# Transposing the normalized activations by DMA instead of TensorE in a hybrid attention and Fourier block

## The chip, the cores and the metric

The kernel runs as one program on all 8 cores of one Trainium2 chip. The time of a run is the device time of the slowest core, in microseconds (us). The cores do not talk to each other: core c computes sequence c of the first batch, and a quarter (2048 tokens) of one of the two longer sequences of the second.

## The reference, cut to what matters

```python
def _mixer_layer(x, ln_w, w_in, q_norm, k_norm, w_f, b_f, w_out):
    h = _rmsnorm(x, ln_w)                              # (B, S, 1024)
    proj = jnp.einsum("bsd,de->bse", h, w_in)          # 1024 -> 2304
    q, k, v, g_a, u_f, g_f = jnp.split(proj, SPLITS, axis=-1)   # 512 128 128 512 512 512
    q = _apply_rope(_rmsnorm(q.reshape(B, S, 8, 64), q_norm), cos, sin)
    k = _apply_rope(_rmsnorm(k.reshape(B, S, 2, 64), k_norm), cos, sin)
    y_attn = _block_attention(q, k, v) * jax.nn.silu(g_a)       # full softmax over S
    y_four = _fourier_mix(u_f, w_f, b_f) * jax.nn.silu(g_f)     # real(fft2), then 128x128 per group
    y = jnp.concatenate([y_attn, y_four], axis=-1)
    return x + jnp.einsum("bse,ed->bsd", y, w_out)
# y_prompt = rmsnorm(_mixer_layer(x_prompt (8, 4096, 1024))), y_sample the same of (2, 8192, 1024)
```

## The kernel before, in words

Each core does two jobs one after the other: job s (S = 8192, its own 2048 query tokens) and job p (S = 4096, all tokens its own). A job has three stages with a barrier between them.

**Pass 1** (L615 to L655) goes over all S tokens in tiles of 128 (64 tiles in job s, 32 in job p), in pairs. Per tile: SP loads 512 KB of x (L623) into one of three buffers xt; ScalarE squares and sums it (L478) and makes the reciprocal root in two tiny steps (L482, L483); VectorE scales it to bf16, hb (L626). The projection needs the model dimension on the partitions, so TensorE transposes hb in eight 128x128 blocks through the identity matrix into a PSUM bank (L631), and VectorE copies the bank to hT (L633). Then eight steps, each a 256-column matmul for K and V (L637) and a 512-column one for the Fourier input U (L640). ScalarE takes U and V out of PSUM (L642, L643). Per pair of tiles the K part goes through `normrope`: square on ScalarE (L498), sum on VectorE (L499), two tiny ScalarE steps (L501, L502), two VectorE products (L503, L506), six GpSimd steps (L517 to L522). TensorE transposes the result, kb (L652, two blocks), and VectorE copies it to kT (L654). GpSimd loads the rotary table of a pair (L618).

**Fourier** (L662 to L716) works from U in SBUF. The change does not touch it.

**Attention** first loads and converts w_out and w_in, then works in chunks of 512 queries (4 in job s, 8 in job p). `part_a` of a chunk normalizes four tiles of x (L797, L480 to L483, L800), transposes them (L809) and copies them (L811) into the four quarters of hTc, of which there is one; projects Q (L814), normalizes and rotates it and transposes it (L825, L829); then makes the gates (L839, exponentials and the reciprocal L847). Job s takes its tiles singly, job p in pairs. `part_b` is the attention itself: per key tile two score matmuls (L864, L866), one exponential of 1024 columns (L872), two value matmuls (L878, L880), and at the end of each of four head pairs a normalization on VectorE and GpSimd (L884 to L892). `part_c` is the output projection (L920), the residual, the last norm and the store (L929). part_a of the next chunk and part_c of the last run as a background stream beside part_b.

**The order of the work** is written by a planner, `Prog.schedule`. The operations of a stage are entered with the buffers that they read and write; each engine's queue is then laid out by a list schedule with fixed charges: it takes the operation that can start first, among equals the one of lower due time, then the one entered first. The emitted queues are run in that order, each engine waiting on semaphores where needed; nothing is reordered on the chip. DMAs are charged on one serial resource for all queues:

```python
if sid == 1 and e == "pe":
    rdy += BG_SLACK                      # 2.0: background TensorE work is planned 2 us late
...
if o.dma:
    xs = max(stt, dma_free)
    dma_free = xs + o.nbytes / 150000.0
    o.t1 = dma_free + 2.0
    free[o.eng] = stt + o.c
```

The charges of compute are n/2400 + 0.03 us on TensorE, (n + 335)/1200 on ScalarE, (n + 150)/960 on VectorE and 0.003 n + 0.15 on GpSimd, with 0.15 us for a hop between engines. A buffer is a whole: a write to any quarter of hTc waits for every read of hTc entered before it. A DMA of a queue also waits for the eighth DMA before it on that queue.

Of the kernel before, what the change touches and what calls it, by code (L numbers as in the profile page):

```python
# [8 lines left out]
BF16 = mybir.dt.bfloat16  # L9
# [5 lines left out]
D = 1024  # L15
# [341 lines left out]
def build(stop=None):  # L357
# [64 lines left out]
    def bank(i, n=1):  # L422
        return psum[:, 512 * i:512 * (i + n)]
# [121 lines left out]
    def run_job(job):  # L545
# [36 lines left out]
        w1 = AF_.get((8, 768), BF16)  # L582
        NXT = 3
        xt = [AF_.get((1024,), F32) for _ in range(NXT)]
        hb = [AF_.get((1024,), BF16) for _ in range(2)]
        hT = [AF_.get((8, 128), BF16) for _ in range(2)]
        junk = AF_.get((1024,), BF16)
        st_s = [AF_.get((4,), F32) for _ in range(2)]
        rt = [AF_.get((2, 64), F32) for _ in range(2)]
# [10 lines left out]
        B_w1, B_U = Buf(), Buf()  # L600
        B_xg = [Buf(), Buf()]
        B_xt = [Buf() for _ in range(NXT)]
        B_hb, B_hT, B_st, B_rt, B_kb = ([Buf(), Buf()] for _ in range(5))
        B_junk = Buf()
        B_p12 = [Buf() for _ in range(NS1)]
        B_stage = [Buf() for _ in range(NSTG)]
# [8 lines left out]
        for jp in range(J // 2):  # L615
            bkv = 2 + (jp % 2)
            rts = jp % 2
            P.op("pool", lambda e, jp=jp, rts=rts: e.dma_start(out=rt[rts], in_=rk[nm][2 * jp:2 * jp + 2].rearrange("t p c -> p t c")),  # L618
                 writes=[B_rt[rts]], dma=True, nbytes=65536)
            for tl in range(2):  # L620
                j = 2 * jp + tl
                xs_, hs = j % NXT, j % 2
                P.op("sp", lambda e, j=j, xs_=xs_: e.dma_start(out=xt[xs_], in_=x_str[j]), writes=[B_xt[xs_]], dma=True, nbytes=524288)  # L623
                ss, lnv, rstd = st_s[hs][:, 0:1], st_s[hs][:, 1:2], st_s[hs][:, 2:3]
                rms_rstd(xt[xs_], B_xt[xs_], junk, B_junk, ss, lnv, rstd, B_st[hs], D)
                P.op("dve", lambda e, xs_=xs_, hs=hs, rstd=rstd: e.tensor_scalar(hb[hs], xt[xs_], rstd, None, ALU.mult),  # L626
                     reads=[B_xt[xs_], B_st[hs]], writes=[B_hb[hs]], n=600)
                bt = j % 2
                psT = bank(bt).bitcast(BF16)
                for kc in range(8):  # L630
                    P.op("pe", lambda e, kc=kc, hs=hs, psT=psT: e.transpose(psT[:, kc * 128:(kc + 1) * 128], hb[hs][:, kc * 128:(kc + 1) * 128], ident),  # L631
                         reads=[B_hb[hs], B_ident], writes=[PB[bt]], n=128)
                P.op("dve", lambda e, hs=hs, psT=psT: e.tensor_copy(hT[hs].rearrange("p a b -> p (a b)"), psT),  # L633
                     reads=[PB[bt]], writes=[B_hT[hs]], n=700)
                bu = 4 + (j % 3)
                for kc in range(8):
                    P.op("pe", lambda e, kc=kc, hs=hs, tl=tl, bkv=bkv: e.matmul(bank(bkv)[:, tl * 256:(tl + 1) * 256], hT[hs][:, kc, :], w1[:, kc, 0:256],  # L637
                                                                       start=(kc == 0), stop=(kc == 7)),
                         reads=[B_hT[hs], B_w1], writes=[PB[bkv]], n=256)
                    P.op("pe", lambda e, kc=kc, hs=hs, bu=bu: e.matmul(bank(bu), hT[hs][:, kc, :], w1[:, kc, 256:768], start=(kc == 0), stop=(kc == 7)),  # L640
                         reads=[B_hT[hs], B_w1], writes=[PB[bu]], n=512)
                P.op("act", lambda e, j=j, bu=bu: e.activation(U[:, j, :], bank(bu), AF.Copy), reads=[PB[bu]], writes=[B_U], n=512)  # L642
                P.op("act", lambda e, j=j, tl=tl, bkv=bkv: e.activation(  # L643
                    vx[:, j, :].rearrange("p (a b) -> p a b", b=64)[:, 0:3:2, :],
                    bank(bkv)[:, tl * 256 + 128:(tl + 1) * 256].rearrange("p (a b) -> p a b", b=64), AF.Copy),
                    reads=[PB[bkv]], writes=[B_vx[j]], n=128)
            ksrc = bank(bkv).rearrange("p (t c) -> p t c", t=2)[:, :, 0:128]
            kslot = jp % 2
            normrope(ksrc, [PB[bkv]], 2, 2, gk, rt[rts], B_rt[rts], kb[kslot], B_kb[kslot], wkk[kslot])
            psK = bank(7).bitcast(BF16)  # L650
            for tl in range(2):
                P.op("pe", lambda e, tl=tl, kslot=kslot, psK=psK: e.transpose(psK[:, tl * 128:(tl + 1) * 128], kb[kslot][:, tl * 128:(tl + 1) * 128], ident),  # L652
                     reads=[B_kb[kslot], B_ident], writes=[PB[7]], n=128)
            P.op("dve", lambda e, jp=jp, psK=psK: e.tensor_copy(kT[:, jp * 256:(jp + 1) * 256], psK[:, 0:256]),  # L654
                 reads=[PB[7]], writes=[B_kT[2 * jp], B_kT[2 * jp + 1]], n=256)  # L655
# [125 lines left out]
        def part_a(ch):  # L781
            P.strm = 1
            cs = ch % 2
            for tp in range(4 // TP):
# [5 lines left out]
                for tl in range(TP):  # L790
                    t = tp * TP + tl
                    tg = ch * 4 + t
                    xs_, hs = cnt["x"] % 2, tg % 2
                    cnt["x"] += 1
                    sts = cnt["st"] % 4
                    cnt["st"] += 1
                    P.op("sp", lambda e, tg=tg, xs_=xs_: e.dma_start(out=xt2[xs_], in_=x_nat[tg]), writes=[B_xt2[xs_]], dma=True, nbytes=524288)  # L797
                    ss, lnv, rstd = st2[sts][:, 0:1], st2[sts][:, 1:2], st2[sts][:, 2:3]
                    rms_rstd(xt2[xs_], B_xt2[xs_], junk2, B_junk2, ss, lnv, rstd, B_st2[sts], D, sq_eng="dve")
                    P.op("dve", lambda e, xs_=xs_, hs=hs, rstd=rstd: e.tensor_scalar(hb2[hs], xt2[xs_], rstd, None, ALU.mult),  # L800
                         reads=[B_xt2[xs_], B_st2[sts]], writes=[B_hb2[hs]], n=600)
                    if TP == 1:
                        ba, bb = 6 + (t % 2), 7 - (t % 2)
                    else:
                        ba = bb = 6 + tl
                    banks.append(bb)
                    psT = bank(ba).bitcast(BF16)
                    for kc in range(8):
                        P.op("pe", lambda e, kc=kc, hs=hs, psT=psT: e.transpose(psT[:, kc * 128:(kc + 1) * 128], hb2[hs][:, kc * 128:(kc + 1) * 128], ident),  # L809
                             reads=[B_hb2[hs], B_ident], writes=[PB[ba]], n=128)  # L810
                    P.op("dve", lambda e, t=t, psT=psT: e.tensor_copy(hTc[:, :, t * 128:(t + 1) * 128], psT.rearrange("p (a b) -> p a b", a=8)),  # L811
                         reads=[PB[ba]], writes=[B_hTc], n=700)
                    for kc in range(8):
                        P.op("pe", lambda e, kc=kc, t=t, bb=bb: e.matmul(bank(bb), hTc[:, kc, t * 128:(t + 1) * 128], w2[:, kc, 0:512], start=(kc == 0), stop=(kc == 7)),  # L814
                             reads=[B_hTc, B_w2], writes=[PB[bb]], n=512)
# [208 lines left out]
```

How the kernel before makes its waits and increments, by code:

```python
                def body(eng):  # L259
                    seen = {}
                    for o in ops:
                        need = {}
                        for d in o.deps:
                            if d.dma:
                                k = ("d",) + d.dsem
                                v = d.dcnt
                                sem = dsem[d.dsem]
                            else:
                                k = ("c", d.eng)
                                v = d.cnt
                                sem = esem[d.eng]
                            if seen.get(k, 0) >= v:
                                continue
                            if k not in need or need[k][1] < v:
                                need[k] = (sem, v)
                        for k, (sem, v) in need.items():
                            eng.wait_ge(sem, v)
                            seen[k] = v
                        ins = o.fn(eng)
                        if o.dma:
                            ins.then_inc(dsem[o.dsem], 16)
                        elif o.sig:
                            ins.then_inc(esem[e], 1)
                    if e == "sp":
                        for k, sem in dsem.items():
                            if dcount[k] > 0:
                                eng.wait_ge(sem, dcount[k])
```

## Time and profile before

| | us |
|---|---|
| median of 2 runs | 3724.66 |
| the two runs | 3652.83, 3796.48 |
| the profiled execution | 3620.57 |
| its span on the slowest core (7) | 3619.0 |
| spans of the 8 cores in it | 3577.8 to 3619.0 |

| engine (core 7) | busy us | share of the span |
|---|---|---|
| TensorE | 2982.6 | 82% |
| ScalarE | 2448.5 | 68% |
| VectorE | 1856.3 | 51% |
| GpSimd | 859.3 | 24% |
| DMA | | mean 45 GB/s |

The profile is of one execution on its slowest core. A group of instructions is named by its source line. "L652 waited for L522" means that the semaphore that released L652 was raised by L522. The granted clock (PEclk) is the TensorE clock as a share of its full speed, 2.4 GHz. Matmuls are pipelined, and their starts are a better guide than their durations: a matmul's record overlaps the next one's.

### The profile page before, as it was taken

To read this page: it belongs to the slowest core of one execution; us is meant where nothing else is said; L and a number is where in the kernel's file an instruction comes from. 1 tells how busy PE (TensorE), PEld (TensorE's weight loads), DVE (VectorE), ACT (ScalarE), POOL (GpSimd) and SP (SyncE) were. 2 spreads that over 40 slices of the span, in tenths; PEclk is the share of its full clock that TensorE was granted. 3 is DMA by queue.
4 is the path that set the end of the run, shared out by engine and by line. 5 is a ranking of instruction groups with operands and counts; after the bars stand their busy time and mean duration, and the time that the engine had idled before them with its cause. 6 is when DMAs were issued, how large, how long until landed. Compare 5 with 4: busy or idle time off the path is not lost.

```text
span 3619.0 us, 51220 instructions; the slowest of 8 cores (3577.8 to 3619.0 us)
## 1 busy us (share of the span) xinstructions
PE 2982.6 (82%) x15376; PEld 1067.2 (29%) x15376; DVE 1856.3 (51%) x2072; ACT 2448.5 (68%) x3409; POOL 859.3 (24%) x1119
## 2 busy tenths in 40 slices
PE   5885651799999999999576642999999999999997
PEld 3553430222222222222143421222222222222221
DVE  3555764633235235311345435765767575757553
ACT  4661220499998998999454640778777878786875
POOL 4556772220002002000145532111111202020100
PEclk8996655899999999999798765999999999988887
DMA  5540005000010010000241023001020111101011
GB/s 153 144 138 14 1 1 156 21 2 1 24 36 14 18 41 13 18 30 1 88 138 48 1 68 99 13 7 65 4 68 30 43 41 32 59 14 59 12 47 35
DMA packets 49547, 162.86 MB, mean 45 GB/s; under 512 B 7088, under 2 KB 9168, under 8 KB 49280
## 3 DMA queue, kind: packets, MB, share of 16 engines
q1 hardware_dynamic: 41536, 138.43, 12.1%
q0 software_dynamic: 7744, 21.15, 2.0%
q8 instruction: 133, 2.18, 0.2%
q14 instruction: 134, 1.10, 0.1%
HBM read 134.39 MB, written 25.17 MB: 44 GB/s over the span
## 4 chain that ended last, share of the span: by engine, by line
PE 64%; DVE 15%; issue 7%; POOL 6%; ACT 4%; DMA 3%; DVEq 0%; POOLq 0%; ACTq 0%; SPq 0%
PE psum L864 16%; PE psum L878 16%; PE psum L880 11%; PE psum L920 5%; DVE arena L847 4%; PE psum L640 3%; PE psum L839 3%; PE psum L814 2%; PE psum L637 2%; DVE arena L676 1%; DVE arena L678 1%; POOL arena L680 1%; POOL arena L682 1%; DMA arena<-w_in 1%; ACT arena L709 1%
## 5 line engine op out<-in xcount | busy, mean ns | idle before, releaser
L872 ACT ACTIVATE arena<-psum 128x1024 bf16<-128x1024 f32 x2048 | 1959.6, 1060 | 296.0 <-PE psum L866 227.3
L878 PE MATMUL psum<-arena 128*128 128x512 bf16 x2048 | 815.6, 399 | 25.4 <-DVE arena L884 24.0
L864 PE MATMUL psum<-arena 64*128 64x512 bf16 x2048 | 794.9, 389 | 49.5 <-ACT arena L872 32.2
L866 PE MATMUL psum<-arena 64*128 64x512 bf16 x2048 | 808.3, 396 | 0.0
L880 PE MATMUL psum<-arena 128*128 128x512 bf16 x2048 | 795.1, 392 | 7.1 <-DVE arena L885 7.0
L864 PEld LDWEIGHTS psum<-arena 64*128 64x128 bf16 x2048 | 188.7, 92 | 952.5 <-issue 950.4
L889 POOL TENSOR_TENSOR arena<-arena 128x512 f32<-128x512 f32 x48 | 59.5, 1239 | 1389.5 <-DVE arena L888 1389.5
L878 PEld LDWEIGHTS psum<-arena 128*128 128x128 bf16 x2048 | 196.2, 96 | 497.1 <-issue 494.6
L847 DVE RECIPROCAL arena<-arena 128x512 f32<-128x512 f32 x96 | 321.7, 3351 | 8.4
L640 PE MATMUL psum<-arena 128*128 128x512 bf16 x768 | 255.3, 381 | 0.0
L637 PE MATMUL psum<-arena 128*128 128x256 bf16 x768 | 208.1, 274 | 54.9 <-DVE arena L633 27.0
L920 PE MATMUL psum<-arena 128*128 128x512 bf16 x768 | 224.3, 403 | 32.8 <-DVE arena L892 17.9
L482 ACT ACTIVATE arena<-arena 128x1 f32<-128x1 f32 x192 | 56.6, 299 | 264.8 <-DVE arena L481 247.4
L700 ACT ACTIVATE arena<-psum 128x256 bf16<-128x256 f32 x192 | 74.9, 390 | 231.7 <-PE psum L692 181.2
L880 PEld LDWEIGHTS psum<-arena 128*128 128x128 bf16 x2048 | 203.3, 100 | 26.4 <-issue 19.9
L839 PE MATMUL psum<-arena 128*128 128x512 bf16 x768 | 199.0, 401 | 8.5 <-DVE arena L493 4.2
L884 DVE COPY arena<-psum 128x512 f32<-128x512 f32 x48 | 32.5, 676 | 323.8 <-PE psum L878 323.8
L517 POOL TENSOR_TENSOR arena<-arena 128x128 f32<-128x128 f32 (+2 forms) x80 | 57.4, 717 | 573.3 <-DVE arena L506 573.3
L866 PEld LDWEIGHTS psum<-arena 64*128 64x128 bf16 x2048 | 189.0, 93 | 7.8 <-issue 7.2
L676 DVE TENSOR_TENSOR arena<-psum,arena 128x512 f32<-128x512 f32 x192 | 133.4, 698 | 106.6 <-PE psum L671 70.4
L671 PE MATMUL psum<-arena 128*64 128x256 bf16 (+1 forms) x1024 | 121.9, 398 | 76.8 <-DVE arena L678 71.7
L927 DVE SCALAR_TENSOR_TENSOR arena<-arena 128x1024 f32<-128x1024 f32 x48 | 61.6, 1283 | 231.1 <-ACT arena L483 230.7
(106 smaller groups left out, 3661.6 us busy)
## 6 DMA issues: line engine op xcount, KB each, us to landing
arena<-xp SPq DMA_DIRECT2D x96, 512.0 KB, 3.8
arena<-xs SPq DMA_DIRECT2D x64, 512.0 KB, 5.2
arena<-xo SPq DMA_DIRECT2D x32, 512.0 KB, 3.6
yp<-arena SPq DMA_DIRECT2D x32, 512.0 KB, 2.7
arena<-w_in POOLq DMA_DIRECT2D x40, 256.0 KB, 5.5
yo<-arena SPq DMA_DIRECT2D x16, 512.0 KB, 2.7
arena<-w_in SPq DMA_DIRECT2D x24, 256.0 KB, 4.8
arena<-w_in SPq DMA_DIRECT2D x16, 128.0 KB, 3.6
```

The costliest lines, as they stand in the source:

```text
L637: P.op("pe", lambda e, kc=kc, hs=hs, tl=tl, bkv=bkv: e.matmul(bank(bkv)[:, tl * 256:(tl + 1) * 256], hT[hs][:, kc, :], w1[:, kc, 0:256], s ...
L640: P.op("pe", lambda e, kc=kc, hs=hs, bu=bu: e.matmul(bank(bu), hT[hs][:, kc, :], w1[:, kc, 256:768], start=(kc == 0), stop=(kc == 7)), rea ...
L671: P.op("pe", lambda e, bl=bl, cl=cl, cidx=cidx, b1=b1: e.matmul(bank(b1)[cl * J:(cl + 1) * J, bl * 256:(bl + 1) * 256], U.rearrange("p j c ...
L676: P.op("dve", lambda e, s1=s1, pv=pv: e.tensor_tensor(p12[s1][:, 0, :, :], pv, t1.unsqueeze(1).to_broadcast([128, 2, 256]), ALU.mult), rea ...
L839: P.op("pe", lambda e, kc=kc, fc=fc, bg=bg: e.matmul(bank(bg), w2[:, kc, 512 + fc * 128:512 + (fc + 1) * 128], hTc[:, kc, :], start=(kc == ...
L847: P.op("dve", lambda e, es=es: e.reciprocal(eg[es], eg[es]), reads=[B_eg[es]], writes=[B_eg[es]], n=3000)
L864: P.op("pe", lambda e, kt=kt, sb=sb, hp=hp: e.matmul(bank(sb), kT[0:64, kt * 128:(kt + 1) * 128], qT[cs][0:64, hp, :], start=True, stop=True),
L866: P.op("pe", lambda e, kt=kt, sb=sb, hp=hp: e.matmul(bank(sb + 1), kT[64:128, kt * 128:(kt + 1) * 128], qT[cs][64:128, hp, :], start=True, ...
L872: P.op("act", lambda e, sb=sb, ps=ps: e.activation(pT[ps], bank(sb, 2), AF.Exp, scale=0.125), reads=[PB[sb], PB[sb + 1]], writes=[B_pT[ps] ...
L878: P.op("pe", lambda e, kt=kt, ps=ps: e.matmul(bank(4), vx[:, kt, 0:128], pT[ps][:, 0:512], start=(kt == 0), stop=(kt == NKT - 1)), reads=[ ...
L880: P.op("pe", lambda e, kt=kt, ps=ps: e.matmul(bank(5), vx[:, kt, 64:192], pT[ps][:, 512:1024], start=(kt == 0), stop=(kt == NKT - 1)), rea ...
L920: P.op("pe", lambda e, c8=c8, half=half, t=t: e.matmul(bank(6 + half), yT[cs][:, c8, t * 128:(t + 1) * 128], wo[:, c8, half * 512:(half + ...
```

## The change

In pass 1 and in part_a, the eight TensorE transposes of a tile and VectorE's copy out of PSUM are replaced by one DMA on SP's queue, SBUF to SBUF, with transposition, 256 KB. In pass 1, hb and hT get three buffers each instead of two (the small statistics buffers keep two). The K and Q transposes (L652, L825) and those of the Fourier stage stay on TensorE. The planner is told nbytes=262144 for each new DMA.

```diff
-        hb = [AF_.get((1024,), BF16) for _ in range(2)]
-        hT = [AF_.get((8, 128), BF16) for _ in range(2)]
+        NHS = 3
+        hb = [AF_.get((1024,), BF16) for _ in range(NHS)]
+        hT = [AF_.get((8, 128), BF16) for _ in range(NHS)]
...
-                bt = j % 2
-                psT = bank(bt).bitcast(BF16)
-                for kc in range(8):
-                    P.op("pe", lambda e, kc=kc, hs=hs, psT=psT: e.transpose(psT[:, kc * 128:(kc + 1) * 128], hb[hs][:, kc * 128:(kc + 1) * 128], ident),
-                         reads=[B_hb[hs], B_ident], writes=[PB[bt]], n=128)
-                P.op("dve", lambda e, hs=hs, psT=psT: e.tensor_copy(hT[hs].rearrange("p a b -> p (a b)"), psT),
-                     reads=[PB[bt]], writes=[B_hT[hs]], n=700)
+                P.op("sp", lambda e, hs=hs: e.dma_start(out=hT[hs], in_=hb[hs].rearrange("p (a b) -> p a b", a=8), transpose=True),
+                     reads=[B_hb[hs]], writes=[B_hT[hs]], dma=True, nbytes=262144)
...
-                    psT = bank(ba).bitcast(BF16)
-                    for kc in range(8):
-                        P.op("pe", lambda e, kc=kc, hs=hs, psT=psT: e.transpose(psT[:, kc * 128:(kc + 1) * 128], hb2[hs][:, kc * 128:(kc + 1) * 128], ident),
-                             reads=[B_hb2[hs], B_ident], writes=[PB[ba]], n=128)
-                    P.op("dve", lambda e, t=t, psT=psT: e.tensor_copy(hTc[:, :, t * 128:(t + 1) * 128], psT.rearrange("p (a b) -> p a b", a=8)),
-                         reads=[PB[ba]], writes=[B_hTc], n=700)
+                    P.op("sp", lambda e, hs=hs, t=t: e.dma_start(out=hTc[:, :, t * 128:(t + 1) * 128], in_=hb2[hs].rearrange("p (a b) -> p a b", a=8), transpose=True),
+                         reads=[B_hb2[hs]], writes=[B_hTc], dma=True, nbytes=262144)
```

## Rows read from the trace of the kernel before

**Rows 1.** Cores: span and mean granted clock of the slowest.
```profile
core 7: 3619.0 us, clock 0.883
```

**Rows 2.** The page's chain of work that ended last, by engine.
```profile
PE 64%; DVE 15%; issue 7%; POOL 6%; ACT 4%; DMA 3%; DVEq 0%; POOLq 0%; ACTq 0%; SPq 0%
```

**Rows 3.** Stretches: start:end length, busy of PE, PEld, DVE, ACT, POOL, PEclk, DMA, GB/s.
```profile
52.00:290.00 238.00, 197.20 (x1511) 123.23 (x1509) 124.44 (x240) 150.53 (x446) 122.26 (x210) 1.00 0.45 133
290.00:545.00 255.00, 151.36 (x1216) 94.86 (x1213) 173.52 (x264) 53.39 (x103) 184.36 (x268) 0.58 0.00 1
...
670.00:1780.00 1110.00, 1068.90 (x4840) 302.68 (x4839) 402.91 (x376) 989.82 (x1125) 99.45 (x114) 0.99 0.06 19
...
1826.00:1956.00 130.00, 101.61 (x767) 62.95 (x765) 61.81 (x121) 73.54 (x218) 61.87 (x110) 0.97 0.31 105
...
2258.00:3619.00 1361.00, 1273.63 (x5668) 377.39 (x5666) 852.33 (x730) 1040.07 (x1227) 193.49 (x160) 0.92 0.11 35
```

**Rows 4.** Timeline of pass 1, 200 to 212 us: start, length, engine, line.
```profile
200.38 0.38 ACT L498 ACTIVATE arena<-psum 128x256 f32<-128x256 f32 x1
...
201.31 0.27 PE L652 MATMUL psum<-arena 128*128 128x128 bf16 x2 [0.77 <-POOL arena L522]
...
202.40 0.30 ACT L501 ACTIVATE arena<-arena 128x4 f32<-128x4 f32 x1 [0.61 <-DVE arena L499]
...
203.17 0.42 DVE L503 TENSOR_TENSOR arena<-psum,arena 128x256 f32<-128x256 f32 x1 [0.86 <-ACT arena L502]
203.26 1.06 PE L631 MATMUL psum<-arena 128*128 128x128 bf16 x16
...
204.59 0.42 DVE L506 TENSOR_TENSOR arena<-arena 128x256 f32<-128x256 f32 x1
...
204.93 0.27 PE L637 MATMUL psum<-arena 128*128 128x256 bf16 x1 [0.61 <-DVE arena L633]
...
205.22 0.45 POOL L517 TENSOR_TENSOR arena<-arena 128x128 f32<-128x128 f32 x1 [3.32 <-DVE arena L506]
...
207.20 0.27 PE L637 MATMUL psum<-arena 128*128 128x256 bf16 x1
...
208.28 0.38 ACT L498 ACTIVATE arena<-psum 128x256 f32<-128x256 f32 x1
...
209.23 0.27 PE L652 MATMUL psum<-arena 128*128 128x128 bf16 x2 [0.78 <-POOL arena L522]
```

**Rows 5.** Groups by line: shapes and count, busy us, mean ns, idle before.
```profile
L478 ACT ACTIVATE arena<-arena 128x1024 bf16<-128x1024 f32 x96 | 101.5, 1057 | 46.1 <-DMA arena<-xp 16.0 <-issue 12.8 <-DMA arena<-xs 8.3
L626 DVE TENSOR_SCALAR arena<-arena 128x1024 bf16<-128x1024 f32 x96 | 76.3, 818 | 9.2 <-ACT arena L483 9.1
L633 DVE COPY arena<-psum 128x1024 bf16<-128x1024 bf16 x96 | 65.6, 687 | 32.5 <-PE psum L631 23.4 <-PE psum L640 8.7
L811 DVE COPY arena<-psum 128x1024 bf16<-128x1024 bf16 x48 | 32.8, 683 | 30.3 <-PE psum L809 19.2 <-PE psum L814 10.8
```

**Rows 6.** Timeline of TensorE after long idle times: pass 1's first tile, then job s's prelude.
```profile
44.66 0.37 PE L637 MATMUL psum<-arena 128*128 128x256 bf16 x1 [10.46 <-DVE arena L537]
...
45.26 0.42 PE L637 MATMUL psum<-arena 128*128 128x256 bf16 x1
...
45.90 0.42 PE L637 MATMUL psum<-arena 128*128 128x256 bf16 x1
...
47.65 0.27 PE L637 MATMUL psum<-arena 128*128 128x256 bf16 x1
...
637.60 3.57 PE L814 MATMUL psum<-arena 128*128 128x512 bf16 x8 [0.68 <-DVE arena L829]
...
654.02 3.57 PE L814 MATMUL psum<-arena 128*128 128x512 bf16 x8 [0.68 <-DVE arena L829]
```

**Rows 7.** DMA: a queue (packets, MB, share of 16 engines), and issues (KB, us to landing).
```profile
q1 hardware_dynamic: 41536, 138.43, 12.1%
...
arena<-xs SPq DMA_DIRECT2D x64, 512.0 KB, 5.2
...
arena<-rq_s POOLq DMA_DIRECT2D x16, 32.0 KB, 2.0
```

More of the change, by code:

```diff
@@ L602, in run_job @@
         B_xt = [Buf() for _ in range(NXT)]
-        B_hb, B_hT, B_st, B_rt, B_kb = ([Buf(), Buf()] for _ in range(5))
+        B_st, B_rt, B_kb = ([Buf(), Buf()] for _ in range(3))
+        B_hb, B_hT = ([Buf() for _ in range(NHS)] for _ in range(2))
         B_junk = Buf()
@@ L621, in run_job @@
                 j = 2 * jp + tl
-                xs_, hs = j % NXT, j % 2
+                xs_, hs = j % NXT, j % NHS
                 P.op("sp", lambda e, j=j, xs_=xs_: e.dma_start(out=xt[xs_], in_=x_str[j]), writes=[B_xt[xs_]], dma=True, nbytes=524288)
-                ss, lnv, rstd = st_s[hs][:, 0:1], st_s[hs][:, 1:2], st_s[hs][:, 2:3]
-                rms_rstd(xt[xs_], B_xt[xs_], junk, B_junk, ss, lnv, rstd, B_st[hs], D)
+                sj = j % 2
+                ss, lnv, rstd = st_s[sj][:, 0:1], st_s[sj][:, 1:2], st_s[sj][:, 2:3]
+                rms_rstd(xt[xs_], B_xt[xs_], junk, B_junk, ss, lnv, rstd, B_st[sj], D)
                 P.op("dve", lambda e, xs_=xs_, hs=hs, rstd=rstd: e.tensor_scalar(hb[hs], xt[xs_], rstd, None, ALU.mult),
-                     reads=[B_xt[xs_], B_st[hs]], writes=[B_hb[hs]], n=600)
-                bt = j % 2
-                psT = bank(bt).bitcast(BF16)
-                for kc in range(8):
-                    P.op("pe", lambda e, kc=kc, hs=hs, psT=psT: e.transpose(psT[:, kc * 128:(kc + 1) * 128], hb[hs][:, kc * 128:(kc + 1) * 128], ident),
-                         reads=[B_hb[hs], B_ident], writes=[PB[bt]], n=128)
-                P.op("dve", lambda e, hs=hs, psT=psT: e.tensor_copy(hT[hs].rearrange("p a b -> p (a b)"), psT),
-                     reads=[PB[bt]], writes=[B_hT[hs]], n=700)
+                     reads=[B_xt[xs_], B_st[sj]], writes=[B_hb[hs]], n=600)
+                P.op("sp", lambda e, hs=hs: e.dma_start(out=hT[hs], in_=hb[hs].rearrange("p (a b) -> p a b", a=8), transpose=True),
+                     reads=[B_hb[hs]], writes=[B_hT[hs]], dma=True, nbytes=262144)
                 bu = 4 + (j % 3)
```

## The prediction, made before the changed kernel had been run

> **What bounds the kernel now.** I read the cores first: core 7 is the slowest, and all views are of it [rows 1]. Then the chain that ended last: two thirds of it is TensorE, a seventh VectorE, almost nothing transfers [rows 2]. An average over a program with six stages says little, so I cut the span by stage [rows 3]. The change touches two kinds of stage. Pass 1 (52 to 290 us for the first job, 1826 to 1956 for the second) has TensorE busy 83% and 78%, the others at most two thirds, DMA a third to under a half. Attention (670 to 1780, 2258 to 3619) has TensorE at 96% and 94% with ScalarE at 89% and 76% close behind.
>
> Then the timeline of pass 1, for one period [rows 4]. A pair of tiles takes 7.90 us (L498 at 200.38 and at 208.28), 3.95 per tile. Eight steps of L637 and L640 come every 0.324 us (204.93 to 207.20 is seven of them), 2.6 us a tile; the eight transposes of a tile are 0.53 (sixteen in 1.06). But TensorE also stops 0.78 us at L652, the two transposes of K, for the last GpSimd step of the rotary chain. That chain is the second bound: from L498 at 200.38 to L652 at 209.23 is 8.85 us, longer than the pair, and it fits only because L652 of one pair stands in TensorE's order behind two whole tiles of the next pair and three steps of a third. The queues are in order, so **where the planner puts L652** decides as much as what TensorE has to do.
>
> **The change part by part.**
>
> *TensorE and VectorE work removed.* Pass 1: 96 tiles lose 0.53 us of transposes, 51 us, and 96 copies by VectorE, 65.6 us [rows 4, 5]. TensorE's two halts behind the copy (0.61 before 204.93) go too. Were nothing else to happen, a tile would go from 3.95 to about 3.3 us. VectorE's copies lie beside TensorE's work except for that halt. Attention: 48 tiles lose 0.53 us (25 us), of which 8 tiles lie in the two preludes where TensorE mostly idles; at most 40 x 0.53 = 21 us are on the path, and of 32.8 us of copies [rows 5] at most 20 more, since VectorE is busy 63% there [rows 3]. The floor is nothing, as ScalarE is near its own limit.
>
> *Transfers added.* 144 transposing DMAs of 256 KB on SP's queue, none of which the trace shows. Latency: between 2.0 us (32 KB load) and 5.2 us (512 KB load) by plain transfers [rows 7]; I take 4. Engine time from below: loads run 133 GB/s at a DMA share of 0.45 [rows 3], 296 GB/s at full share, so 0.9 us. From above: if each 256-byte piece (128 rows x 8 blocks, 1024 pieces) cost what a packet now does, 0.121 x 3619 x 16 / 41536 = 0.169 us [rows 7], it is 1024 x 0.169 / 16 = 10.8 us. I take about 1.5, near the byte end, because the pieces are an order smaller than the packets priced; both ends stay for the range. A tile's load takes 0.45 x 3.95 = 1.8 us of the DMA engines, so 3.3 per tile in all, which fits under a tile's period.
>
> The Trainium skill speaks with two voices on that price. "VectorE: DVE Perf Modes", The three transpose paths, gives 1309 ns for 128x128 by DMA against 390 by TensorE; eight in a row would be 10.5 us a tile, an estimate from that page. "Advanced Engine Details and Errata", X-Bar Transpose (TRN2), has them about as fast as plain DMAs, 350 to 400 GB/s, an estimate of 0.7 us a tile. The first would make the DMA rival below true, the second would leave my sum alone; no row here decides.
>
> *SP's queue.* In pass 1 the transpose of tile j waits for L626 of tile j; behind it stands the load of tile j+3, which waits for the same L626 to free its buffer. It loses only the issue. Three hb and three hT buffers allow a transpose a latency of over one period. The loop through the three xt buffers (load 5.2, L478 1.26 with its accumulator read, two tiny steps 0.5, L626 0.8, issues about 1) is 8.8 us for three tiles [rows 5, 7], hidden under 11.8 us. In attention each transpose also waits until L814 of the tile before has read hTc, since hTc is one buffer; y stores and xt2 loads stand behind that wait. Cover: SP is far ahead there. For the second job's prelude, two pairs expose about 3 us each, +6; the first job's hides under the 16.4 us between tiles (L814 at 637.60 and 654.02) [rows 6].
>
> *The planner.* This is the term I trust most. It charges each DMA bytes/150000 us on one serial resource plus 2.0 to land. These figures set only the order. Before: per tile TensorE is charged 0.67 + 3.04 + 0.08 = 3.79, DMA 3.50 + 0.22 = 3.72, so it plans TensorE-bound. After: TensorE 3.12, DMA 3.50 + 1.75 + 0.22 = **5.47**, so it plans DMA-bound, tiles 5.47 apart with TensorE idle between. Take the pair's second tile to start at 0. Its K is complete at 2.8; evacuations (0.39, 0.71), L498 (0.49), L499 (0.42) follow; L478 of a later tile, landed at 3.5, gets in on ScalarE (1.13), L501 and L502 with one small step between end at 6.5; L503, L626 of a later tile, L506 end at 8.3; six GpSimd steps of 0.53 end at 11.8, L652 is ready at 11.9. The next two tiles start at 5.5 and 10.9. So L652 goes behind one tile and about 1 us of the second (two to four of eight steps), where it now goes behind two tiles and three steps. Nothing on the chip is as slow as the plan's DMA, but the order remains: the chain now covers with 2.6 + 0.8 = 3.4 us of TensorE work, not 7.9.
>
> *Price of that.* Real chain after the change, from rows: 8.85 [rows 4], less 0.6 because L499 no longer waits for the late copy behind L652 (L501 started 202.40, ScalarE was free near 201.8), with L633 (0.69) before L506 exchanged for L626 (0.82) [rows 5]: about 8.3. Before it, from the last L637's end (207.47) to L498 (208.28), 0.81. Behind it, the two K transposes cost 0.1 and the remaining 5.5 steps 5.5 x 0.324 = 1.8 before the next pair's K is complete. Period 8.3 + 0.8 + 0.1 + 1.8 = **11.0 us a pair** for 7.90: +3.1 x 48 = +149 us. With L652 ahead of the tile, or L478 out of the chain, I get 10.5, +125.
>
> *Clock.* TensorE would then stand still 9.1 - 3.4 = 5.7 us in one piece per pair. Rows for that: in pass 1 the granted clock is 1.00, at 59% busy in the first Fourier stage 0.58 [rows 3]. After 10.46 us of idling, steps come every 0.64 us, the 1.2 GHz level, and by 47.65 are back at the 2.4 GHz one; L814 in the prelude after long idles takes 3.57 for eight, also the low level [rows 6]. The work right behind the stall is what the loop contains, so at the low level it costs 5.5 x 0.64 = 3.5 in place of 1.8 and the pair 12.8 us: +4.9 x 48 = +235. I take the clock as fallen in most pairs, 12.3 us, **+211 us**; ends +125 and +235.
>
> *Sum.* Pass 1 +211 (all removals are inside the new period). Attention between -40 and +10, I take -15. Total +196 on the profiled execution's 3620.6 us: 3817. That execution lies 32 us under the lower of the two runs (3652.8) and 104 under their median (3724.66); for a run like the lower, 3850. The forecast's own range is 3740 to 3900.
>
> **Rivals.**
>
> *Faster: the order holds.* If L652 stays about two tiles behind its chain, pass 1 drops to 3.3 us a tile (-62), attention gives 25 to 40: 3620 - 95 = 3525, or 3555 as a run. For: every removed instruction sits on the bounding engine. Against: the chain of 8.3 + 0.8 us does not shrink, and the planner's 5.47. It decides if L652 has over 6 us of TensorE work ahead of it. Chance 0.15.
>
> *No difference.* L652 falls deep enough that the pair stays near 8 us (about six steps into the tile with the clock up), or the gain in attention repays half of a small loss: 3600 to 3700. Chance 0.15.
>
> *Slower by the DMA engines.* If a transpose takes over 12.3/2 - 1.8 = 4.4 us of them, pass 1 goes at 1.8 + T a tile. At 10.8: (12.6 - 3.95) x 96 = +830, 4450; in attention the planner allows 3.75 + 0.15 + 2.0 = 5.9 us, so a latency near 12.8 stops TensorE up to 6.9 us in 44 tiles, +300 more. For: packet price [rows 7] and small pieces. Against: bytes. At T = 6 it gives +370, 3990. Chance 0.25, most of it between 3900 and 4450.
>
> The change not doing what it says is no rival: the edit has no path left with a TensorE transpose of hb.
>
> **Chances.** Forecast 0.45, DMA-bound 0.25: slower by over 2% (about what a measurement tells from no change) 0.70. Same 0.15, faster 0.15. Range 3620 to 4400: it leaves out about 0.12 below and 0.08 above.
>
> **What would show it.** Right: after, L652 follows one tile and a few steps; its wait on GpSimd L522 grows from 0.8 to about 5 us and heads TensorE's waits; pass 1 goes at 11 to 13 us a pair with the granted clock under 1.00 and TensorE near 50 to 80% busy; L631 and L809 are gone; transposes land in 3 to 6 us. Wrong: TensorE waiting instead at L637 for the transposing DMA (then the DMA rival), or pass 1 at 7 to 8 us a pair. Attention should hardly move; if it grows by tens of us, transposes land later than 5.9 us.

## The result and the profile after

The changed kernel is slower. The ratio to before is **1.035, 95% interval 1.026 to 1.045**. The median of all its 12 runs is 3871.8 us, that of 10 runs of before 3614.5 us. In most runs of the changed kernel, the profiled one among them, the cores of one die or both had a lower granted clock and took longer, so every ratio here is of runs without such cores, and profiles are compared on cores of a die without them: cores 0 to 3 in these two. All rows below are of core 0 unless said.

The cores of the changed kernel (span, mean granted clock), then those of before:

```profile
core 0: 3711.0 us, clock 0.883
...
die 0 (median of its cores): 3716.3 us, clock 0.882
die 1 (median of its cores): 3835.7 us, clock 0.815
```

```profile
core 0: 3585.0 us, clock 0.903
...
die 0 (median of its cores): 3582.6 us, clock 0.903
```

On core 0 the change costs 126 us, by the median of cores 0 to 3 it costs 134. Where the 126 us lie is read from the first and last start of a few lines (duration min/median/max, first to last start). Changed kernel: L635 is the K/V projection, L669 the first Fourier matmul, L858 the scores.

```profile
L635 PE MATMUL psum<-arena x768: 269/273/422, 47.7 to 2080.4; 128*128 128x256 bf16 x192
L669 PE MATMUL psum<-arena x1024: 271/417/521, 407.2 to 2244.4; 128*64 128x256 bf16 x86, 128*32 128x256 bf16 x85
L858 PE MATMUL psum<-arena x2048: 372/373/631, 770.9 to 3667.4; 64*128 64x512 bf16 x187
```

Its timeline of SP's queue, the first weight load of job p:

```profile
1875.50 1.77 SPq L529 DMA_DIRECT2D arena<-w_in  x4
```

The same lines of before (L637, L671, L864):

```profile
L637 PE MATMUL psum<-arena x768: 269/273/421, 46.3 to 1946.6; 128*128 128x256 bf16 x192
L671 PE MATMUL psum<-arena x1024: 272/417/537, 308.2 to 2109.9; 128*64 128x256 bf16 x86, 128*32 128x256 bf16 x85
L864 PE MATMUL psum<-arena x2048: 372/373/627, 668.1 to 3540.3; 64*128 64x512 bf16 x187
```

And its first weight load of job p:

```profile
1786.25 1.76 SPq L529 DMA_DIRECT2D arena<-w_in  x4
```

Job s's pass 1 ends 99.0 us later (407.2 for 308.2). Job p begins 89.3 later, so job s's Fourier and attention gave 9.7 back. Job p's pass 1 ends 133.8 later, so it lost 44.6. The end is 126 later: 7.8 back. Pass 1 **+143.6**, everything else **-17.6**.

Stretches of the changed kernel that answer to [rows 3] (busy of PE, PEld, DVE, ACT, POOL, PEclk, DMA share, GB/s): pass 1 and attention of job s, then of job p.

```profile
52.00:391.00 339.00, 224.13 (x1018) 113.71 (x1038) 90.53 (x181) 155.60 (x454) 113.10 (x210) 0.81 0.64 144
...
765.00:1873.00 1108.00, 1047.73 (x4655) 297.56 (x4748) 399.12 (x370) 986.26 (x1127) 100.11 (x118) 0.99 0.07 22
...
1922.00:2092.00 170.00, 107.31 (x505) 55.06 (x517) 42.27 (x88) 70.69 (x207) 58.11 (x110) 0.80 0.53 127
...
2390.00:3711.00 1321.00, 1205.49 (x5349) 358.69 (x5456) 836.11 (x703) 1026.48 (x1228) 192.70 (x163) 0.97 0.14 42
```

In pass 1 TensorE is now 66% and 63% busy where it was 83% and 78%, at a granted clock of 0.81 and 0.80 where it was 1.00 and 0.97. No other engine is near its limit, and the DMA engines are 64% busy. The program is waiting, and the timeline says for what. It answers to [rows 4]; L650 is what L652 was, L629 what L626 was, L641 takes V out of PSUM, and L620 is the rotary table's load:

```profile
201.96 0.27 PE L635 MATMUL psum<-arena 128*128 128x256 bf16 x1 [0.40 <-ACT arena L641]
...
207.13 0.37 PE L650 MATMUL psum<-arena 128*128 128x128 bf16 x2 [4.04 <-POOL arena L522]
207.29 0.42 PE L635 MATMUL psum<-arena 128*128 128x256 bf16 x1
...
209.85 0.42 PE L635 MATMUL psum<-arena 128*128 128x256 bf16 x1
...
211.29 0.38 ACT L498 ACTIVATE arena<-psum 128x256 f32<-128x256 f32 x1
211.55 1.06 ACT L478 ACTIVATE arena<-arena 128x1024 bf16<-128x1024 f32 x1
...
212.59 0.29 ACT L501 ACTIVATE arena<-arena 128x4 f32<-128x4 f32 x1
...
213.35 0.42 DVE L503 TENSOR_TENSOR arena<-psum,arena 128x256 f32<-128x256 f32 x1 [1.17 <-ACT arena L502]
...
213.69 0.74 DVE L629 TENSOR_SCALAR arena<-arena 128x1024 bf16<-128x1024 f32 x1
214.35 0.42 DVE L506 TENSOR_TENSOR arena<-arena 128x256 f32<-128x256 f32 x1
...
214.40 0.27 PE L635 MATMUL psum<-arena 128*128 128x256 bf16 x1 [0.30 <-ACT arena L641]
...
218.84 0.27 PE L650 MATMUL psum<-arena 128*128 128x128 bf16 x2 [3.31 <-POOL arena L522]
```

The tile that starts at 201.96 gets three steps done, TensorE stands 4.04 us for the rotary chain, and its last five steps (207.29 to 209.85 are five starts) come every 0.64 us, the 1.2 GHz level. Only then is the pair's K complete and the next chain begins (L498 at 211.29), with L478 and L629 of a later tile inside it. Between them stands one whole tile, then three steps from 214.40, and TensorE waits again. The rotary table's loads, one per pair, give the mean period: (274.94 - 127.52) / 13 = 11.34 us, for (275.27 - 124.56) / 19 = 7.93 before.

```profile
127.52 0.74 POOL L620 DMA_DIRECT2D arena<-rk_s  x1
...
274.94 0.74 POOL L620 DMA_DIRECT2D arena<-rk_s  x1
```

```profile
124.56 0.75 POOL L618 DMA_DIRECT2D arena<-rk_s  x1
...
275.27 0.75 POOL L618 DMA_DIRECT2D arena<-rk_s  x1
```

These are TensorE's waits at the K transposes and for transposing DMAs over the whole changed kernel (us in total, times, longest). Before, the wait at L652 was 46.2 us in 45 times:

```profile
PE psum L650 <- POOL arena L522: 162.3, 47, 6.2
...
PE psum L808 <- DMA arena<-arena: 6.6, 2, 3.3
...
PE psum L635 <- DMA arena<-arena: 3.8, 2, 3.6
...
PE psum L638 <- DMA arena<-arena: 2.9, 1, 2.9
```

It waits for a transposing DMA three times in pass 1 (L635, L638; 6.7 us) and twice in attention (L808, the Q projection; 6.6 us). These transfers land in a median of 3.4 us, and make 1056 packets each, (193600 - 41536) / 144, against [rows 7]. From the page of the profile, which is of the slowest core (4):

```profile
q1 hardware_dynamic: 193600, 176.20, 17.4%
...
arena<-arena SPq DMA_TRANSPOSE x144, 3.4
```

### The profile page after: what moved, and what is told of

Same layout as the page of the kernel before. It is cut to its first block, busy times and chain, and to the rows that moved or that the text cites. A ratio compares the mean times of both kernels' runs of the same rounds, so it can differ in the third digit from the quotient of the medians.

```text
span 3842.0 us, 49251 instructions; the slowest of 8 cores (3711.0 to 3842.0 us)
## 1 busy us (share of the span) xinstructions
PE 3106.6 (81%) x14224; PEld 1012.5 (26%) x14224; DVE 1765.6 (46%) x1928; ACT 2493.5 (65%) x3409; POOL 837.2 (22%) x1119
## 3 DMA queue, kind: packets, MB, share of 16 engines
q1 hardware_dynamic: 193600, 176.20, 17.4%
## 4 chain that ended last, share of the span: by engine, by line
PE 61%; DVE 14%; issue 8%; POOL 7%; ACT 5%; DMA 4%; DVEq 0%; POOLq 0%; SPq 0%; ACTq 0%
PE psum L858 16%; PE psum L872 15%; PE psum L874 11%; PE psum L914 5%; DVE arena L841 5%; PE psum L638 3%; PE psum L808 3%; PE psum L833 2%; PE psum L635 2%; POOL arena L680 1%; POOL arena L678 1%; DVE arena L676 1%; DVE arena L674 1%; ACT arena L707 1%; DMA arena<-w_in 1%
## 5 line engine op out<-in xcount | busy, mean ns | idle before, releaser
L866 ACT ACTIVATE arena<-psum 128x1024 bf16<-128x1024 f32 x2048 | 1998.9, 1036 | 248.5 <-PE psum L860 216.7
L872 PE MATMUL psum<-arena 128*128 128x512 bf16 x2048 | 848.3, 414 | 18.1 <-DVE arena L878 17.4
L858 PE MATMUL psum<-arena 64*128 64x512 bf16 x2048 | 835.2, 408 | 30.9 <-ACT arena L866 17.7
L874 PE MATMUL psum<-arena 128*128 128x512 bf16 x2048 | 837.8, 410 | 27.2 <-DVE arena L879 27.1
L860 PE MATMUL psum<-arena 64*128 64x512 bf16 x2048 | 842.5, 412 | 0.0
L858 PEld LDWEIGHTS psum<-arena 64*128 64x128 bf16 x2048 | 188.7, 92 | 1000.2 <-issue 999.2
L638 PE MATMUL psum<-arena 128*128 128x512 bf16 x768 | 355.5, 491 | 1.8 <-DMA arena<-arena 1.8
L635 PE MATMUL psum<-arena 128*128 128x256 bf16 x768 | 257.1, 338 | 78.6 <-issue 43.0
L914 PE MATMUL psum<-arena 128*128 128x512 bf16 x768 | 232.9, 408 | 28.9 <-DVE arena L886 17.9
L833 PE MATMUL psum<-arena 128*128 128x512 bf16 x768 | 201.3, 403 | 18.2 <-DVE arena L842 11.9
L808 PE MATMUL psum<-arena 128*128 128x512 bf16 x384 | 108.6, 434 | 127.6 <-DVE arena L537 118.1
L641 ACT ACTIVATE arena<-psum 128x128 bf16<-128x128 f32 x96 | 26.5, 276 | 284.8 <-PE psum L635 284.8
L669 PE MATMUL psum<-arena 128*64 128x256 bf16 (+1 forms) x1024 | 120.8, 394 | 78.6 <-DVE arena L676 74.3
```

The source lines that it names most:

```text
L669: P.op("pe", lambda e, bl=bl, cl=cl, cidx=cidx, b1=b1: e.matmul(bank(b1)[cl * J:(cl + 1) * J, bl * 256:(bl + 1) * 256], U.rearrange("p j c ...
L833: P.op("pe", lambda e, kc=kc, fc=fc, bg=bg: e.matmul(bank(bg), w2[:, kc, 512 + fc * 128:512 + (fc + 1) * 128], hTc[:, kc, :], start=(kc == ...
L858: P.op("pe", lambda e, kt=kt, sb=sb, hp=hp: e.matmul(bank(sb), kT[0:64, kt * 128:(kt + 1) * 128], qT[cs][0:64, hp, :], start=True, stop=True),
L860: P.op("pe", lambda e, kt=kt, sb=sb, hp=hp: e.matmul(bank(sb + 1), kT[64:128, kt * 128:(kt + 1) * 128], qT[cs][64:128, hp, :], start=True, ...
L866: P.op("act", lambda e, sb=sb, ps=ps: e.activation(pT[ps], bank(sb, 2), AF.Exp, scale=0.125), reads=[PB[sb], PB[sb + 1]], writes=[B_pT[ps] ...
L872: P.op("pe", lambda e, kt=kt, ps=ps: e.matmul(bank(4), vx[:, kt, 0:128], pT[ps][:, 0:512], start=(kt == 0), stop=(kt == NKT - 1)), reads=[ ...
```

## The experiments

All are of the whole kernel on 8 cores; periods of a pair are from the rotary loads between 120 and 280 us, as above. "Steps behind" counts the L637 steps between a pair's end and its K transposes in TensorE's queue: 19 before, 11 in the changed kernel. An edit shifts the lines of a kernel, so the same operation can have another number in each.

**The order without the transfers (e1).** The kernel before, with one number of the planner changed:

```diff
-  ... x_str[j]), writes=[B_xt[xs_]], dma=True, nbytes=524288)
+  ... x_str[j]), writes=[B_xt[xs_]], dma=True, nbytes=786432)
```

> The kernel before, TensorE transposes and all; only the planner's charge for a tile's x load in pass 1 is raised from 524288 to 786432 bytes, which is what load and transposing DMA are charged together in the changed kernel. No transposing DMA runs. Laid out so, the K transposes stand 8 steps of L637 behind their pair in most of job s, where the kernel before has 19. Order theory: the wait of TensorE for the last GpSimd step grows from 0.8 to 3 us or more in most pairs, a pair goes from 7.9 to 11 to 12.5 us, the profiled undisturbed core ends 100 to 190 us later than before's 3585. Rival (it is the transposing DMA itself, its latency or its use of the DMA engines): a pair stays at 7.9, time within 0.5% of before.

Ratio to before 1.022, interval 1.018 to 1.026; core 0 at 3665.4, 80 us later than before's 3585.0. A pair takes (269.87 - 123.85) / 14 = 10.43 us. Its stretch 120 to 280 us and TensorE's waits in it:

```profile
120.00:280.00 160.00, 105.54 (x749) 63.34 (x762) 69.19 (x123) 84.86 (x235) 57.24 (x111) 0.98 0.33 106
```

```profile
PE psum L652 <- POOL arena L522: 20.7, 15, 2.0
PE psum L631 <- DVE arena L626: 17.4, 16, 1.1
PE psum L637 <- DVE arena L633: 14.2, 15, 0.9
```

With no transposing DMA anywhere, an early place of the K transposes costs 2.5 us per pair, and the rival falls. But the amount missed my range: I had one wait of 3 us, and there are three of 1.4, 1.1 and 0.9. The 2.5 is not a share of the changed kernel's 3.4 us either, since this is a third order: the K transposes stand 8 steps behind their pair and not 11, and L478 of a later tile comes after L502 and not inside the chain, which takes 6.6 us from L498 to L652. With its halts in short pieces the clock stays at 0.98. That is the first hint that a part of the changed kernel's loss is the clock.

**The transfers without the order (e2).** The changed kernel, K transposes planned later:

```diff
+        o.lag = lag                      # op(..., lag=0.0)
...
+                        rdy += o.lag
...
-   reads=[B_kb[kslot], B_ident], writes=[PB[7]], n=128)
+   reads=[B_kb[kslot], B_ident], writes=[PB[7]], n=128, lag=6.0)
```

> The changed kernel; only the K transposes of pass 1 are planned 6 us later on TensorE (a lag added to their ready time, as the background stream has its slack). They then stand 22 steps behind their pair in place of 11. All transposing DMAs stay. Order theory: the stall before them goes, a pair goes from 11.0 us to 6.5 to 7.5, pass 1 is shorter than before the change, and the whole is 150 to 200 us under the changed kernel, 20 to 80 us under before (ratio to before 0.98 to 0.995). Rival (DMA): a pair stays over 10 us, TensorE waits for the transposing DMA at L635 instead, ratio to before stays at 1.03.

Ratio 0.992, interval 0.990 to 0.995; core 0 at 3557.9, 153 us under the changed kernel. Every one of the 144 transfers is still there. The pair takes (277.76 - 125.07) / 20 = 7.63 us, just over my range. The wait at the K transposes is gone, the clock is back at 0.98, and a new pattern stands there:

```profile
120.00:280.00 160.00, 120.41 (x706) 66.53 (x717) 60.62 (x128) 108.06 (x317) 78.60 (x147) 0.98 0.97 217
```

```profile
PE psum L637 <- DMA arena<-arena: 26.8, 23, 3.0
```

The DMA engines are 97% busy and TensorE now waits for the transposing DMAs (L637 is this kernel's K/V projection).

**The change in halves.** Pass 1 alone (e3: part_a's lines of before put back), and attention alone (e4: pass 1's put back).

> The change made in pass 1 alone; attention's part_a keeps TensorE transposes and VectorE copies. Order theory: all of the loss, so about +140 to +150 us over before on the undisturbed core (ratio 1.035 to 1.045), 10 to 20 us slower than the changed kernel. Rival (part of the loss is the attention's transfers): clearly less than the changed kernel's loss.

> The change made in attention's part_a alone; pass 1 as before. Forecast of the sum: -15 us, ends -40 and +10 (ratio 0.989 to 1.003); from the changed kernel's trace about -18. Rival: attention loses too when pass 1 does not hide it, ratio over 1.005.

Pass 1 alone: 1.044, interval 1.035 to 1.053, cores 3728.7 to 3737.5. Attention alone: 0.9935, interval 0.9905 to 0.9965, core 0 at 3561.7. So all of the loss is in pass 1, and the same transfer is a gain of about 20 us in the stage where the planner's order does not turn against it.

**Another charge instead of a lag (e5).** The changed kernel, the planner told 262144 bytes for the x load and 65536 for the transposing DMA in pass 1, nothing else:

```diff
-  ... x_str[j]), writes=[B_xt[xs_]], dma=True, nbytes=524288)
+  ... x_str[j]), writes=[B_xt[xs_]], dma=True, nbytes=262144)
...
-  reads=[B_hb[hs]], writes=[B_hT[hs]], dma=True, nbytes=262144)
+  reads=[B_hb[hs]], writes=[B_hT[hs]], dma=True, nbytes=65536)
```

> The changed kernel, every instruction kept, but the planner is told 262144 bytes for a tile's x load and 65536 for its transposing DMA in pass 1, so that it plans TensorE-bound (3.12 us a tile) and not DMA-bound. Laid out so, the K transposes stand 20 to 24 steps behind their pair. Order theory: no lag is needed, the right charge alone brings a pair from 11.3 to 7.4 to 8.0 us, bounded by 1.6 + 2.0 us of the DMA engines per tile; whole time within 1% of e2 (ratio to before 0.985 to 1.000). Rival (it was the lag's other effects that helped e2): ratio over 1.015.

Ratio 0.992, interval 0.989 to 0.996; a pair takes (277.06 - 125.42) / 20 = 7.58 us. Two numbers that the chip never sees, and core 0 ends at 3555.4, 156 us under the changed kernel.

**Only K later, on the kernel before (e6).** The control of the lag, same edit as above on the old kernel:

> The kernel before (TensorE transposes everywhere), only its K transposes of pass 1 planned 6 us later, 31 to 34 steps behind their pair in place of 19. Theory: the 0.78 us halt per pair is all that this can give, so a pair goes from 7.9 to 7.1 us, 48 pairs give 37 us, ratio to before 0.988 to 0.993. Rival (the order was already good, the next wait takes its place): within 0.3% of before.

The lower two of its runs are 3549.2 and 3550.0 beside 3590 to 3593 for before on the same chip, 41 us or 1.1% less, and core 0 is at 3545.5; a pair takes (266.97 - 119.30) / 21 = 7.03 us. As expected: the old kernel's order was itself not right. It also means that e2's gain over before was the lag's: with TensorE transposes the same lag gives 7.03 us a pair, with transposing DMAs 7.63.

**What the clock costs (e7).** The changed kernel with TensorE kept at work in the stall:

```diff
             normrope(ksrc, ...)
+            for _f in range(10):
+                P.op("pe", lambda e: e.matmul(bank(0), w1[:, 0, 0:128], w1[:, 0, 0:512], start=True, stop=True),
+                     reads=[B_w1, wkk[kslot]["buf"]["xf"]], writes=[PB[0]], n=512)
```

> The changed kernel with ten extra matmuls of 512 columns per pair in pass 1, into a PSUM bank that nothing reads, that become ready when the rotary chain reaches GpSimd; they run inside TensorE's stall of about 4 us and the K transposes stay 11 steps behind their pair. Clock theory: TensorE's halts are then no longer than about 2 us each, the granted clock in pass 1 rises from 0.80 to above 0.9, the five steps behind the stall take 1.6 us in place of 3.2, and a pair goes from 11.2 to about 9.6 us: 50 to 80 us faster than the changed kernel. Rival (the clock does not matter there, or added work only adds time): as slow as the changed kernel or slower by up to 2.1 us a pair.

The median span of cores 4 to 7 is 3651.8 us, 64.5 less than the changed kernel's 3716.3 (its cores 0 to 3). More work, less time. On core 5 the ten matmuls (L650 here) sit in the stall. L499 and L479 are here what L498 and L478 were, L654 is the K transposes; the rows show two chains, one from 170.98 and one from 200.69:

```profile
170.98 0.38 ACT L499 ACTIVATE arena<-psum 128x256 f32<-128x256 f32 x1
171.25 1.06 ACT L479 ACTIVATE arena<-arena 128x1024 bf16<-128x1024 f32 x1
...
174.62 2.32 PE L650 MATMUL psum<-arena 128*128 128x512 bf16 x10 [1.62 <-DVE arena L507]
178.46 0.27 PE L654 MATMUL psum<-arena 128*128 128x128 bf16 x2 [0.55 <-POOL arena L523]
...
200.69 0.38 ACT L499 ACTIVATE arena<-psum 128x256 f32<-128x256 f32 x1
...
202.93 1.05 ACT L479 ACTIVATE arena<-arena 128x1024 bf16<-128x1024 f32 x1
...
207.27 0.27 PE L654 MATMUL psum<-arena 128*128 128x128 bf16 x2 [0.35 <-POOL arena L523]
```

```profile
120.00:280.00 160.00, 129.13 (x732) 67.86 (x732) 49.61 (x100) 85.23 (x252) 60.50 (x113) 1.00 0.76 172
```

The granted clock is 1.00 for 0.80, a pair (274.51 - 119.87) / 16 = 9.67 us for 11.34. Not all of the 1.67 is the clock, because the filler also made the planner lay ScalarE's queue out otherwise. Between 120 and 280 us:

| pairs | chain, L498 (L499) to K transposes | from there to the next L498 (L499) | period |
|---|---|---|---|
| changed kernel, 13 pairs, L478 inside the chain | 7.52 | 3.82 | 11.34 |
| filler, 7 pairs, L479 inside, as at 170.98 | 7.46 | 2.49 | 9.94 |
| filler, 9 pairs, L479 after the chain's small steps, as at 200.69 | 6.60 | 2.85 | 9.45 |

The first two rows have the same chain. What differs is the stretch behind it, where the five steps stand: 1.3 us less. At most it is five steps at 0.324 instead of 0.64, 1.6 us; in some pairs the first steps behind the halt still came every 0.324 us and the clock fell only after them (three steps from 241.88 in the changed kernel). So of the 3.41 us that a pair lost, about 1.4 is the clock that fell (11.34 - 9.94), and 2.0 is the order (9.94 - 7.93). The other 0.3 that this run gained is ScalarE's order.

**Is the DMA's capacity a wall in the changed kernel?** Half of each x tile's load taken away (the right half is a constant, K, V and U are not the reference's; the planner's charge stays), in the changed kernel (e10) and in e2 (e8b):

```diff
-  e.dma_start(out=xt[xs_], in_=x_str[j])
+  e.dma_start(out=xt[xs_][:, 0:512], in_=x_str[j][:, 0:512])
```

> The changed kernel with the left half of each x tile loaded in pass 1 only and the right half a constant (K, V and U are not the reference's); queue orders unchanged, K transposes 11 steps behind. It takes 0.8 us of the DMA engines off each tile. Order theory: the changed kernel's pass 1 has the DMA engines 0.67 busy and nothing waits for them, so a pair stays at 11.2 to 11.4 us and the whole within 10 us of the changed kernel's 3711 to 3722 on undisturbed cores. DMA rival: a pair drops by 1 us or more, 50 us or more in all.

> The kernel e2 (all transposing DMAs, K transposes later) but pass 1 loads only the left half of each x tile, the right half is a constant, so K, V and U are not the reference's. It takes 256 KB per tile off the DMA engines and leaves every other instruction. In e2 the DMA engines are 97% busy and a pair takes 7.45 us. DMA-wall theory (load about 1.6 us and transposing DMA about 2.0 us of all engines per tile): per tile 0.8 + 2.0 = 2.8, TensorE 2.7, so a pair goes to 6.0 to 6.7 us with the DMA share falling to 0.85 to 0.95, and pass 1 is 40 to 60 us shorter than e2's. Rival (the latency of the transposing DMA, or the rotary chain, is the wall): a pair stays over 7.2 us.

e10: cores 3711.5 to 3722.8, a pair (278.17 - 128.29) / 13 = 11.53 us. The DMA share falls from 0.67 to 0.45 and nothing gets faster, so the rival falls for the kernel as it is.

e8b, one run: core 0 at 3544.5, 13 us under e2, a pair (275.33 - 120.57) / 21 = 7.37 us for 7.63. My expectation of 6.0 to 6.7 failed. The DMA share fell as it should,

```profile
120.00:280.00 160.00, 126.13 (x729) 69.67 (x743) 61.73 (x130) 110.56 (x322) 82.36 (x154) 0.97 0.78 149
```

and TensorE still waits for the transfers (in this kernel L639 is the K/V projection and L635 the transposing DMA):

```profile
PE psum L639 <- DMA arena<-arena: 19.8, 18, 2.6
```

```profile
207.87 1.23 SPq L635 DMA_TRANSPOSE arena<-arena  x1
...
212.17 0.27 PE L639 MATMUL psum<-arena 128*128 128x256 bf16 x1 [1.61 <-DMA arena<-arena]
```

From the issue to the first matmul it is 4.3 us although the engines are 78% busy and no longer 97%, and SP issues as soon as VectorE has made hb. So capacity held e2 back by no more than 0.26 us a pair, and right behind it stands the transfer's latency; what in the order keeps hb from being made earlier, I did not separate.

**Versions meant to beat both.** Hybrid (e9): in pass 1 even tiles by DMA (charged 131072 bytes), odd ones by TensorE, lag 3.0 for the K transposes (23 steps behind), attention by DMA.

> A version meant to beat both: in pass 1 the first tile of a pair is transposed by DMA and the second by TensorE, with the K transposes planned later (23 steps behind their pair), attention's transposes by DMA as in the changed kernel. Per pair the DMA engines then have 2 x 1.6 + 2.0 = 5.2 us and TensorE 5.2 + 0.5 + 0.1 = 5.8 us. If both walls are as measured a pair takes 6.3 to 6.9 us: 50 to 75 us off pass 1 and 18 off attention, ratio to before 0.975 to 0.983. Rival: the waits of two unlike tiles add up and a pair stays at 7.4 us or more, ratio 0.988 or more.

Ratio **0.983, interval 0.981 to 0.984**; four runs from 3526.4 to 3532.7. A pair takes (260.25 - 124.91) / 19 = 7.12 us, over my 6.9, and the whole time is at the edge of what I expected.

TensorE transposes in all of pass 1 with the K transposes later, attention by DMA (e11 with a lag of 6 us, e12 with 2):

> Candidate: pass 1 as before with TensorE transposes and the K transposes planned 6 us later (e6, a pair 7.03 us), attention's transposes by DMA (e4, about 20 us less). If the two gains add: 3549 - 20 = 3529 us, the same as e9's 3528 to within 6, which would mean that transposing by DMA in pass 1 is worth nothing once the K transposes stand right. Rival: e9 is clearly faster, or the sum is over 3540.

> e11 with a lag of 2 us in place of 6: the K transposes stand 24 steps behind their pair. The chain needs about 8 us after the pair's last K matmul and 24 steps with 16 to 24 transposes are 8.5 to 9.5 us of TensorE work, so the halt should be gone as in e11, and the stage's end, where e11 waits 6 us for the last pair, is shorter by some 3 us per job: 0 to 10 us faster than e11. Rival: halts of some tenths of a us remain, 0 to 15 us slower.

Lag 6: 0.981, interval 0.973 to 0.988, profiled cores 3519.6 to 3529.1, a pair (265.40 - 126.18) / 20 = 6.96 us. Lag 2: 0.982, interval 0.974 to 0.989, cores 3519.0 to 3530.2, 7.06 us. e11 is the sum that was expected; e12 was not faster, and its wait for the last pair of job s is no shorter (6.8 us for 6.0). The three cannot be told apart. So transposing half of pass 1 by DMA (e9) is worth nothing once the K transposes stand right. Transposing all of it (e2, core 0 at 3557.9 beside e11's 3529.1) costs 29 us even then. In attention the DMA is worth its 20 us.

## Why the prediction was right, and where it was off

**The mechanism, by its own steps, was right.** The planner becomes DMA-bound in its own books, the K transposes move to one tile and two to four steps behind their pair (measured: one tile and three), the halt at L522's consumer grows from 0.8 us to about 5 (measured 2.7 to 4.0 in most pairs; the longest, 6.2, is the last pair of a job, which waited 7.0 before) and heads TensorE's waits, the clock falls. Undoing the order (e2, e5) takes the loss away with all transfers kept; an early place of the K transposes alone (e1) costs 80 us without any.

**The size was too large, mostly in one term.** Pass 1 was priced at +211 us and measured +143.6, under the price that was taken though inside its ends of +125 and +235. Per pair: forecast 11.0 at full clock and 12.8 at the low level, taken 12.3; measured 9.94 at full clock with the same chain (e7) and 11.34. The clock's part was right: 1.3 was taken, 1.8 if it fell in every pair, and 1.4 measured. What was mis-sized is the chain, and with it the order's part: 3.1 forecast, 2.0 measured. From L498 to the K transposes I had 8.3 us, and it is 218.84 - 211.29 = 7.55, after 8.85 before. The sum exchanged VectorE's copy L633 (0.69) for L626 (0.82) between L503 and L506, and so let that stretch grow by 0.13. But the copy had also waited for TensorE's transposes inside the chain:

```profile
203.98 0.69 DVE L633 COPY arena<-psum 128x1024 bf16<-128x1024 bf16 x1 [0.39 <-PE psum L631]
```

That wait went too: L506 starts 1.00 us behind L503 (213.35, 214.35) where it was 1.42 (203.17, 204.59). That is 0.55 of the missing 0.8. And five steps were left behind the stall, not five and a half. Last, 3.41 us x 48 pairs would be 164 us; the 20 us between that and 143.6 lie in the first and last pairs of each job, which lost less than the steady ones, and the sum charged all 48 alike.

**Attention** was priced at -15 between -40 and +10; -17.6 in the changed kernel, about -20 alone (e4).

**The transfer's price** was taken as 1.5 us of the engines between 0.9 and 10.8. From the DMA shares I estimate 0.67 x 5.67 = 3.80 us per tile less 1.62 for the load (0.41 x 3.96), about 2.2, and 1.8 to 2.1 in the kernels with half the load, if half a load costs half. So near 2 us. The packets number 1056 where 1024 pieces were supposed, and each costs far less than the packets of [rows 7], 2 x 16 / 1056 = 0.03 us beside 0.169: the price per packet does not carry from 3.3 KB to 256 bytes. Of the two estimates from the Trainium skill, 10.5 us by "VectorE: DVE Perf Modes", The three transpose paths, is far out as a price for eight blocks in one transfer, and 0.7 us by "Advanced Engine Details and Errata", X-Bar Transpose (TRN2), is a third of what is measured; both bear on the chance of the DMA rival, and the truth lay by the cheap one.

**The DMA rival** (from 4.4 us of engines per tile) did not decide, e10 shows it. It is real one step further: with the order mended a tile takes 0.97 x 3.82 = 3.7 us of the DMA engines in e2, and 0.91 x 3.79 = 3.4 in e5, beside the 3.5 us that a whole tile takes in e6. So by this estimate the engines leave nothing to win in pass 1. They are not the only wall, for with half the load (e8b) a pair still takes 7.37 us beside e6's 7.03. I had set the transfer's price against a pair of 12.3 us only, and not against the best pair. The faster rival's 3.3 us a tile was reached in no order that was tried; with all transfers kept the best is 3.79 (e5).

**The stated time**, 3850, lies near the median of all 12 runs, 3872, and that is luck. The sum said +196 us for the profiled execution, and on core 0 the change costs 126. What brings the median up is not in the sum.

## What to carry to other kernels

In a kernel whose queues are laid out ahead by charges, price a new operation twice: what it costs the chip, and what its charge does to everybody else's place in the queues. Look for a long chain that returns to an in-order engine, count the work that stands ahead of its return, and compare that with the chain's length; here 19 steps covered it and 11 did not. And look at what follows a halt on TensorE: behind the changed kernel's halts of 2.7 to 4.0 us all or most of the next steps ran at the lower clock level, and as five of them were on the loop, each halt cost more than its length. Behind the halts of 0.9 to 1.4 us of e1 the steps came at full rate.

## What the runs showed of the hardware

- A DMA with transposition of a 128x1024 bf16 tile, SBUF to SBUF: 1056 packets, 3.4 us to landing at the median, about 2 us of all 16 engines (an estimate from the DMA shares above, 1.8 to 2.2), and 1.24 us of SP's queue (L631 at 214.62 in the changed kernel), where a plain load of 512 KB takes 0.47 (L625 at 216.01).
- TensorE's granted clock in pass 1, 120 to 280 us: with 66% busy in the records and one halt of 2.7 to 4.0 us per pair (the changed kernel) it was 0.80; with 66% busy and halts of 1.4, 1.1 and 0.9 us (e1) it was 0.98; with the halt filled in its middle (e7, 81% busy) it was 1.00. So the share of busy time does not tell the clock. Whether the length of the halts does, these runs do not separate: part of the changed kernel's busy time is steps at half speed, so e1 did more work in its 66%.
